# The down projection of a conv-gated MLP, turned token by token

## The reference

```
h = h + concat(lru, attention) @ w_out
u = rmsnorm(h, ln_ffn)
g_up, v_up = split(u @ w_up)                 # 1024 -> 2 x 3072
g_up = causal_dwconv(g_up, ffn_conv_w, ffn_conv_b)   # 3 taps along the tokens
h = h + (gelu(g_up) * v_up) @ w_down         # 3072 -> 1024
gate = sigmoid(rmsnorm(h, ln_ple) @ w_ple_gate)
h = h + gate * (p @ w_ple_proj)
```

## Time and profile before

| | |
|---|---|
| median of 3 timed runs | 637.48 us |
| the profiled execution | 639.78 us |
| its span, first to last instruction | 637.8 us |
| busy: PE, DVE, POOL, ACT | 632.8, 435.4, 357.3, 350.4 us |

### The profile page before, as it was taken

One profiled execution on the slowest core, in us unless ns is written; L12 is line 12 of the kernel. 1 busy time (PEld: TensorE's weight loads), 2 busy tenths in 40 slices (PEclk: granted clock), 3 DMA queues, 4 the chain that ended last, 5 costly groups with the idle time before them and its releaser, 6 DMA issues.

```text
span 637.8 us, 8982 instructions
## 1 busy us (share of the span) xinstructions
PE 632.8 (99%) x3357; PEld 545.6 (86%) x3357; DVE 435.4 (68%) x687; ACT 350.4 (55%) x537; POOL 357.3 (56%) x288
## 2 busy tenths in 40 slices
PE   8999999999999999999999999999999999999997
PEld 6887788888888888889988888899888888998886
DVE  3583399978748796877734468677344686788574
ACT  5859953878837455465423345654243456576331
POOL 5674443644307537588645455886444558855370
PEclk9999999999999999999999999999999999999999
DMA  8733334471103315267732323677233226773022
GB/s 300 282 124 108 98 100 120 115 221 38 62 1 110 122 34 165 99 144 167 185 101 99 100 99 100 144 171 181 100 100 99 100 100 150 168 179 130 33 84 83
DMA packets 24954, 78.38 MB, mean 123 GB/s; under 512 B 2896, under 2 KB 3536, under 8 KB 24912
## 3 DMA queue, kind: packets, MB, share of 16 engines
q1 hardware_dynamic: 21168, 68.12, 33.9%
q0 software_dynamic: 3456, 9.44, 7.8%
q10 hardware_dynamic: 288, 0.27, 0.2%
HBM read 62.74 MB, written 2.10 MB: 102 GB/s over the span
## 4 chain that ended last, share of the span: by engine, by line
PE 99%; DMA 1%; DVE 0%; issue 0%
PE psum L1405 30%; PE psum L1407 30%; PE psum L1406 30%; PE psum L1601 2%; PE psum L1587 1%; PE psum L1547 1%; PE psum L1451 1%; PE psum L1454 1%; PE psum L1459 1%; DMA lead<-in_lead_in 1%; PE psum L1517 1%; PE psum L1502 0%; PE psum L1568 0%; PE psum L1444 0%; PE psum L1544 0%; DVE fin L1376 0%
## 5 line engine op out<-in xcount | busy, mean ns | idle before, releaser
L432 POOL TENSOR_TENSOR wlo<-raw,whi 128x512 fp32r<-128x512 f32 x82 | 114.0, 1390 | 192.7 <-ACT whi L521 192.3
L1406 PE MATMUL psum<-ulo,whi 128*128 128x512 f32 x488 | 189.9, 389 | 0.0
L1405 PE MATMUL psum<-uhi,whi 128*128 128x512 f32 x488 | 189.9, 389 | 0.0
L1407 PE MATMUL psum<-uhi,wlo 128*128 128x512 f32 x488 | 189.8, 389 | 0.0
L433 POOL TENSOR_TENSOR wlo<-raw,whi 128x512 fp32r<-128x512 f32 x82 | 114.0, 1390 | 0.0
L521 ACT ACTIVATE whi<-raw 128x1024 fp32r<-128x1024 f32 x78 | 81.9, 1053 | 54.1 <-PE psum L1407 53.4
L1406 PEld LDWEIGHTS psum<-ulo,whi 128*128 128x128 f32 x488 | 91.6, 188 | 19.1
L1407 PEld LDWEIGHTS psum<-uhi,wlo 128*128 128x128 f32 x488 | 91.6, 188 | 19.0
L1405 PEld LDWEIGHTS psum<-uhi,whi 128*128 128x128 f32 x488 | 91.6, 188 | 18.9
L1279 DVE TENSOR_TENSOR res<-res,psum 128x512 f32<-128x512 f32 x72 | 48.4, 685 | 33.8 <-PE psum L1407 32.1
L763 ACT ACTIVATE tmp<-psum,vec 128x512 f32<-128x512 f32 x24 | 16.6, 690 | 72.7 <-DVE psum L1200 72.7
(11 more groups left out here) (241 smaller groups left out, 1302.2 us busy)
## 6 DMA issues: line engine op xcount, KB each, us to landing
raw<-in_weights SPq DMA_DIRECT2D x106, 512.0 KB, 3.3
xlo<-ws POOLq DMA_DIRECT2D x24, 384.0 KB, 6.0
res<-in_x_t SPq DMA_DIRECT2D x8, 256.0 KB, 6.9
xtok<-in_x SPq DMA_DIRECT2D x4, 512.0 KB, 9.1
raw<-in_weights SPq DMA_DIRECT2D x7, 256.0 KB, 7.4
out<-fin SPq DMA_DIRECT2D x7, 256.0 KB, 2.0
k_more<-kT SPq DMA_DIRECT2D x6, 256.0 KB, 4.8
kT<-kT SPq DMA_DIRECT2D x3, 256.0 KB, 4.1
```

The lines of the kernel that those rows point to most:

```text
L432: nc.gpsimd.tensor_tensor(wlo[s][:, 0:CW // 2], raw[s][:, 0:CW // 2], whi[s][:, 0:CW // 2].bitcast(F32), ALU.subtract)
L1405: mm(o, ahi, bhi, start=start, stop=False, skip_group_check=shared)
L1406: mm(o, ahi, blo, start=False, stop=False, skip_group_check=shared)
L1407: return mm(o, alo, bhi, start=False, stop=stop, skip_group_check=shared)
```

## The change

The down stage is laid out the other way round. The activation sums (128 tokens of a block) stand in PE and 512 output channels of weight sums move; the result has tokens on partitions and is kept in `tok`, starting from zero. Work goes product by product: 14 units a phase, unit (o, q) is product o with the pairs 2q and 2q+1, 12 matmuls of 512 columns; each product has two banks of its own, eight banks for four products in turn.

- Weight blocks: four blocks (W00, W11, W10, W01) of two chunks each a phase. W00 and W11 go to four new buffers `held`, loaded at up chunks 9 and 10; W10 and W01 go through the ring behind the last up chunk.
- Weight sums: ten units a phase need one, each 128x1024. POOL makes the two of unit 2 and 5 (`pool_sum`), DVE the other eight (`weight_sum`), in the down stage.
- Splits: ACT one copy of 128x1024 a unit (`unit_high`); POOL subtracts the low parts of units 0 to 7 (`unit_low`); for units 8 to 13 ACT makes a negated copy and POOL issues a DMA that adds the sum onto it (`unit_add`, 512 KB).
- DVE adds each finished product to `tok` (`give`), 15 operations a phase.
- `res` is written out to the output tensor in the first up stage and read back to `back` at the start of the third down stage. At the end PE turns `tok` by 32 transposes of 128x128 (`turn_back`), DVE adds `back` (`add_back`) into `h3`, which takes the place of `res` behind.

The diff, cut to its core:

```
+PRODUCTS = ((T3, W00, None, None), (T4, W11, None, None), (T1, W00, W11, ALU.add), (B22, W10, W00, ALU.add),
+            (T7, W10, W11, ALU.subtract), (B11, W01, W11, ALU.add), (T6, W01, W00, ALU.subtract))
+GIVES = (((1, 1), (3, 1)), ((0, -1), (2, -1)), ((0, 1), (3, 1)), ((1, 1), (0, -1)), ((0, 1),), ((2, 1), (3, -1)), ((3, 1),))
+UNITS = [(0, 0), (1, 0), (2, 0), (0, 1), (1, 1), (2, 1)] + [(o, q) for o in range(3, 7) for q in range(2)]
+LOW_UNITS = 8
+POOL_SUMS = 2
 # POOL
+            def unit_low(ph, u):
+                pool.wait_ge(d_hi, N_UNITS * ph + u + 1)
+                nc.gpsimd.tensor_tensor(low[:, 0:CW // 2], whole[:, 0:CW // 2], high[:, 0:CW // 2].bitcast(F32), ALU.subtract)
+                nc.gpsimd.tensor_tensor(low[:, CW // 2:CW], whole[:, CW // 2:CW], high[:, CW // 2:CW].bitcast(F32),
                                         ALU.subtract).then_inc(d_lo, 1)
+            def unit_add(ph, u):
+                pool.wait_ge(d_neg, (N_UNITS - LOW_UNITS) * ph + u - LOW_UNITS + 1)
+                pool.dma_start(unit_slot(u)[1][:, :], ws[SUM_UNITS.index(u) % RING][:, :],
+                               accum_op=ALU.add).then_inc(x_low[u % RING], 16)
...
+                pool_sum(ph, 0)
+                for u in range(LOW_UNITS):
+                    if u == 4:
+                        pool_sum(ph, 1)
+                    unit_low(ph, u)
+                for u in range(LOW_UNITS, N_UNITS):
+                    unit_add(ph, u)
 # ACT: units 0 to 3 stand between the taps and GeLUs of the last pair, then
                     act_pair(pair)
+                for u in range(RING, N_UNITS):
+                    unit_high(ph, u)
+                if ph < PHASES - 1:
+                    for s in range(RING):
+                        hi_part(C_UP + PH_CHUNKS * (ph + 1) + s, s)
 # DVE
+            def weight_sum(ph, n):
+                u = SUM_UNITS[n]
+                if n < 4:
+                    dve.wait_ge(act_lo, 2 * PH_PAIRS * (ph + 1) - 1)
+                elif n < 8:
+                    dve.wait_ge(d_lo, LOW_UNITS * ph + SUM_UNITS[n - 4] + 1)
+                else:
+                    dve.wait_ge(x_low[n - 8], added(ph, n))
...
+                V.tensor_tensor(ws[n % RING][:, :], source(a, q)[:, :], source(b, q)[:, :], op).then_inc(w_sum, 1)
...
                     pair_sums(pair)
                     low_plain(pair)
+                weight_sum(ph, 2)
                 low_sums(pair)
+                weight_sum(ph, 3)
+                weight_sum(ph, 4)
+                weight_sum(ph, 5)
+                give(ph, 0)
+                weight_sum(ph, 6)
+                give(ph, 1)
+                weight_sum(ph, 7)
+                give(ph, 2)
+                weight_sum(ph, 8)
+                weight_sum(ph, 9)
+                give(ph, 3)
+                give(ph, 4)
...
+            add_back(0)
+            add_back(1)
+            give(PHASES - 1, 5)
+            low_ple(0)
+            low_ple(1)
+            add_back(2)
+            add_back(3)
             low_ple(2)
             low_ple(3)
+            give(PHASES - 1, 6)
 # PE
+            def unit(ph, u):
+                if q == 0 and o < 4:
+                    pe.wait_ge(f_conv, 16 * ph + (12, 12, 14, 16)[o])
+                    pe.wait_ge(t_ok, 5 * (last_pair + o // 2))
+                elif q == 0:
+                    pe.wait_ge(d_step, GIVEN[6] * ph + GIVEN[o - 4])
+                if u < LOW_UNITS:
+                    pe.wait_ge(d_lo, LOW_UNITS * ph + u + 1)
+                else:
+                    pe.wait_ge(x_low[u % RING], added(ph, u))
+                for k in range(2):
+                    pair = 2 * q + k
+                    pe.wait_ge(act_lo, 2 * (PH_PAIRS * ph + pair) + (1 if x < 2 else 2))
+                    w = slice(k * T, (k + 1) * T)
+                    for j in range(2):
+                        t = slice(j * P, (j + 1) * P)
+                        last = three(mbank[2 * (o % 4) + j][:, :], ahi[:, pair, x, t], alo[:, pair, x, t], high[:, w], low[:, w],
+                                     pair == 0, pair == 3)
+                last.then_inc(unit_done, 1)
...
             for t in range(TT):
-                last = project(C_PP % RING, t, mbank[t][:, :], slice(0, T))
+                if t == 2:
+                    pe.wait_ge(d_step, GIVEN[6] * PHASES)
+                    pe.wait_ge(h_ok, 4)
+                    for m in range(4, KD):
+                        turn_back(m)
+                last = project(C_PP % RING, t, gbank[t][:, :], slice(0, T))
 # SP
+                    if ph == 0 and i == 8:
+                        sp.wait_ge(res_add, KD)
+                        sp.dma_start(out[:, :, :], res[:, :, :]).then_inc(res_moved, 16)
+                    if i in (9, 10):
+                        for q in range(2):
+                            load_held(ph, i - 9, q)
+                for block in (W10, W01):
+                    for q in range(2):
+                        load_ring(ph, block, q)
```

More of the change, by code:

```diff
@@ new lines, in _, with give @@
+            written = {}
+            given = [0]
+            def give(ph, o):
+                dve.wait_ge(unit_done, N_UNITS * ph + PRODUCT_UNITS[o])
+                if ph == 0 and o == 0:
+                    dve.wait_ge(res_moved, 16)
+                    dve.wait_ge(sqr, KD)
+                first = 2 * (o % 4)
+                for idx, sign in GIVES[o]:
+                    m, h = divmod(idx, 2)
+                    for tiles in ([slice(0, 2)] if o % 4 != 2 else [slice(0, 1), slice(1, 2)]):
+                        b = (3, 0, 2, 6)[o % 4] if tiles.start == 0 else 5
+                        wide = tiles.stop - tiles.start
+                        src = psum[:, 512 * b:512 * (b + wide)].rearrange("p (t w) -> p t w", w=T)
+                        dst = tok[:, 2 * h + tiles.start:2 * h + tiles.stop, m * T:(m + 1) * T]
+                        if ph == 0 and o < 2:
+                            ins = V.tensor_scalar(dst, src, float(sign), None, ALU.mult)
+                        else:
+                            dve.wait_ge(d_step, written[idx])
+                            ins = V.tensor_tensor(dst, dst, src, ALU.add if sign > 0 else ALU.subtract)
+                        ins.then_inc(d_step, 1)
+                        given[0] += 1
+                    written[idx] = given[0]
@@ L1735, in _, with turn_back @@
+            def turn_back(m):
+                for j in range(TT):
+                    last = nc.tensor.transpose(turn_bank[m][:, j * P:(j + 1) * P], tok[:, j, m * P:(m + 1) * P], ident[:, :])
+                last.then_inc(turned, 1)
             for pair in range(2, PH_PAIRS):
@@ L1737, in _ @@
             for ph in range(PHASES):
-                for n in range(KD * ph, KD * (ph + 1)):
-                    down(n)
+                for u in range(N_UNITS):
+                    if ph == PHASES - 1 and u == 12:
+                        pe.wait_ge(d_step, GIVEN[6] * ph + GIVEN[4])
+                        turn_back(0)
+                        turn_back(1)
+                    if ph == PHASES - 1 and u == 13:
+                        turn_back(2)
+                        turn_back(3)
+                    unit(ph, u)
                 if ph < PHASES - 1:
```

405 lines of the change are left out of this document (194 added, 211 removed).

## The result

| | before | after |
|---|---|---|
| median, us | 637.61 (636.54 to 637.88, 4 runs) | 658.86 (658.16 to 659.24, 4 runs) |
| span of the profiled execution | 637.8 | 656.3 |
| its own time | 639.78 | 658.16 |

The change makes the kernel slower: the ratio is 1.0328 (95% interval 1.0311 to 1.0345), 21.25 us, where 15.5 were forecast (653.0, range 641 to 662). The time lay in the range, and the direction had the chance of 0.85.

A forecast was written before the change was run, and what follows sets the result against it. PE, busy 99% of the span, was taken to bound the kernel, every wait lost in full. -6.75 + 3.5 + 3 x 6.05 + 0.65 = +15.5 us gave 653.0 us beside the median of 637.48, range 641 to 662.

The forecast's parts named there:

- PE's own sum: On PE: 504 matmuls of 512 columns for 1008 of 256 save 6.75 us; 32 turns at the end add 3.5.
- Rival (d): Down matmuls on PE: at a gap of 0.240 for 512 columns the 6.75 us are gone; 660 us, chance 2%.
- The chain in turns: Down stage: DVE and POOL alternate on SBUF operations, low 7b ends at 22.5; units 5 to 7 wait 1.7, 0.95, 0.9 us.
- The first add: Unit 8's accumulating DMA, issued at 22.5 us into the stage, lands in 5.3 us; unit 8 waits 2.5 us.
- The four waits: PE's waits at units 5 to 8 of each down stage: 6.05 us a phase, making the stage 44.1 for 40.3.
- Behind it all is early: Units after 8 never wait: the DMAs of DVE's sums 8 and 9 land at 36.6 and 38.7, due 38.8 and 41.5.
- The two large transfers: Writing res out and reading it to back, 2 MB each, costed at nothing; without cover some 7 us each.
- The tail: After the third down stage: the last 16 turns wait for give(6) until 49.4, costing 0.65 us.
- (a): POOL keeps pace in the down stage and waits vanish: 634.9 us; 10% faster, 5% within 0.2%, 5% for 639 to 643.
- (b): PE's clock falls behind its waits in the down stages: +2.7 us a phase, +8, 661 us; chance 10%.
- (c): The adds land late, each with the longest time of 8.6: three such cost 3.3 us more each, 663 us; chance 8%.
- The price from the page: The skill's 2.0 us plus bytes over 436e3 for unit 8's add, 3.2 us: wait 0.4, sum 6 us lower; not adopted.

The follow-up runs named there:

- experiment 9: Against the kernel before: the change with POOL's and ACT's early work moved ahead, adds only at units 9 and 11, each issued between halves of a POOL subtraction; 638.53 us.
- experiment 6: The change with POOL's and ACT's work for units 4 and 5 earlier, adds of 512 columns, DVE's sums for units 8 to 13 of 64; 637.79 us, ratio 0.9998.
- Experiment 4: The change with each adding DMA covering 512 of 1024 columns (work left out), timed against the kernel before; 646.70 us, ratio 1.0133.
- experiment 3: The change with the four ring loads behind each down stage bringing 64 of 1024 columns (work left out), against the kernel before; 652.38 us, ratio 1.0222.
- experiment 1: The change with POOL's second sum and ACT's high parts of units 4 and 5 made earlier, against the kernel before; 654.21 us, ratio 1.0247.
- experiment 2: The change with DVE's weight sums for units 8 to 13 covering 64 of 1024 columns (work left out), against the kernel before; 650.78 us, ratio 1.0197.
- experiment 5: The change with earlier POOL and ACT work, low_sums before DVE's first weight sum, POOL subtracting units 8, 10, 12, adds at 9, 11, 13; 644.06 us, ratio 1.0082.
- experiment 7: The change with POOL's and ACT's work for units 4 and 5 earlier and adds of 512 columns, DVE's sums whole; 640.49 us, ratio 1.0040.

## Why the prediction was right, point by point

- **Direction and cause: right.** PE had no slack, and the feeders of units 5 to 8 came late by turns between DVE and POOL. PE's list names POOL's low parts for units 5 to 7, three times each, and the first add is what unit 8 waits for.
- **PE's own sum, -6.75 + 3.5: right.** Down matmuls start 0.227 apart. In experiment 9 all that exceeds this pace, from start to start, is 1.1 us in the second down stage, 1.5 in the third and 0.5 ahead of the last turns, listed waits and late starts together. With 3.5 for the turns and the first stage like the second, that makes -6.75 + 3.5 + 2 x 1.1 + 1.5 + 0.5 = +0.95, beside +0.98 measured and +1.3 between the two traces. Rival (d), a wide matmul that is no cheaper, needed 6.75 more in experiments 6 and 9, and is out.
- **The chain in turns: right in order, 0.6 to 1.0 too long at its end.** Behind the stage's start at 415.44, sum 2 ended at 6.45 (forecast 6.5), low 4b at 10.1 (10.4), low 5b at 14.6 (15.2), low 6b at 18.0 (18.85), low 7b at 21.5 (22.5). A wide sum and a half together were priced at 1.15 + 1.25 = 2.40 us and took 2.24 to 2.27; which of the two was oversized the rows don't say. Units 5 to 7 lost 2.55 us a stage from start to start (forecast 3.55).
- **The first add: right, a little long.** It landed in 4.6 to 4.8 us (forecast 5.3), and unit 8 lost 1.8 to 2.0 us, not 2.5. The four waits together are 4.4 to 4.6 us a stage and not 6.05: 4.5 us too many in the run.
- **"Behind it all is early": the step that failed.** The prediction let the adds of units 9 to 13 land like the first. They took, in order of issue in the second stage, 6.6, 8.9, 9.8, 10.1 and 10.1 us. It took room on the DMA engines for granted: it looked at their share for the two large transfers alone, and the 0.65 of the down stage in the earlier trace rows is a mean over a stretch in which the adds were spread out (those for the third stage were issued from 11.6 us ahead of its start to 28.4 behind it). Here six go out in its second half, each with 2.9 us of all engines, together with two ring loads. That was in reach before the run: the number of adds in the second half was known, only their engine time was not, and the prediction priced a landing and not the queue of six. It cost 3.1 us in the second stage and some 10 in the run. The adds were not late in being issued (unit 12's at 30.1 us, where the forecast had its sum ready at 29.1), they were slow to land. Experiment 4 (fewer bytes in the adds) took these waits away in the first two stages and left 0.4 us from start to start at unit 9 in the third, experiment 3 (fewer bytes beside them) in the second stage and for the larger part in the others, and neither touched the order of anything. In the third stage the load of p (512 KB, issued 23.8 us behind the start) goes out beside the adds too; there add 9 took 8.5 us and not 6.6, and unit 9 waited as well. That this load is the reason was not tested.
- **The sum by stages.** With units alone a stage takes 38.1. The first two took 46.7 and 45.8, which leaves 8.6 and 7.7 us of losses, and from the third start to the gate it was 55.06 against 38.1 + 5.46 + 3.5, which leaves 8.0. Together 24.3, where 18.15 + 0.65 were forecast: -6.75 + 3.5 + 24.3 = 21.05, beside 21.25 measured. So two errors partly met: -4.5 for the four first waits, and some +10 for what comes behind. That is luck: with the four waits as large as forecast, the rest would have carried the time to some 663 us, over the end of the range.
- **The two large transfers, priced at nothing: right.** All 19 waits listed for the change behind 6 us stand in the down stages, and `back` landed 8.2 us behind its issue at the third stage's start, 13 us before the first add.
- **The tail: small, as forecast.** The last turns start 0.52 us behind the matmul ahead of them and not 0.227, so 0.3 us for give(6), forecast 0.65. In experiment 9, 1.72 us pass from the start of the last 16 turns to the next matmul, as the 1.75 of the earlier trace rows said.
- **Rivals.** (a) did not happen, and experiment 9 shows that it would have needed another order on POOL; even then the time is not under before's, and the 634.9 us that (a) forecast were not reached in experiment 6 either (637.79). (b) did not happen in the change itself, with waits of up to 1.8 us at a clock of 1.00 throughout. It did once each in experiment 1, where PE waited 1.39 and then 2.66 us and the clock stood at 0.88 and 0.78 behind, in experiment 2, behind a wait of 1.91, and in experiment 5, behind one of 2.01. Each time it cost some 1.6 us, where (b) had 2.7 a phase. The Trainium skill (TensorE: Matmul & The Clock Gate, Why this matters for your kernels) advises against gaps for this reason, and these three traces agree. The length of the wait alone does not decide it: waits of 2.14 and 2.04 us in experiment 1 and of 2.0 in experiment 7 left the clock at 1.00. (c) is the half that came true: not each first add landed late, but each later one.
- **The price from the page.** The 3.2 us that the Trainium skill's fit gives (DMA: Bandwidth & Descriptors, Anatomy of one DMA) for 512 KB was under every landing of an adding DMA of that size here, 4.5 us at the least. The plain loads of 512 KB, issued by SP, landed in 3.3 us at the median.

## What to carry to other kernels

Where an engine is busy without a gap, a cheaper instruction on it is worth only what its feeders can keep up with: write down for every unit when it is due, and for every feeder when it is done, to the end of the stage and not only to the first wait. Price DMAs that go out together by the engine time they take (bytes times their own cost), summed over the stretch in which they must land, and not by the landing of one of them nor by a mean share. And count units from a known start before you name the one that waits: one such slip cost an experiment here, and the cure for the right one, one issue moved by 2 us, was worth 5.45 us.

## What the runs showed of the hardware that was not expected

- An adding DMA from SBUF to SBUF holds the 16 DMA engines for 2.9 us per 512 KB, and a load of 512 KB in the same window for 1.3: more than twice per byte.
- Behind a wait of PE the first matmul's record is 0.47 to 0.50 us long and not 0.39, and the next start comes 0.31 to 0.34 behind it and not 0.227. The late start is there also behind delays that no list shows (unit 10 of the second stage, 447.33).
- The clock fell behind waits of 1.91, 2.01 and 2.66 us and did not behind others of 2.0 to 2.14. Behind each, seven matmuls in a row started 0.43 us apart and not 0.227, which cost 1.6 us.
- The record of a DMA issue on POOL is 0.84 to 1.35 us long, POOL's next instruction starts 0.6 us behind its start (experiment 9: 428.55, 429.16), and the issue stands in line behind POOL's own wait for its turn with DVE.
